# Second mixer of a two-block kernel: one projection chunk moved ahead of the low-rank matmuls, weight splits moved ahead of the token shifts, four small pieces of arithmetic moved between engines

## The reference

```python
h = rms_norm_2(x, mix_norm[l])
p = h @ w_in[l]                                  # 256 x 5296
p_rwkv = token_shift(p[..., :SHIFT_COLS], shift_mu[l])   # u + (prev - u) * mu
# inside rwkv7_mixer, on the shifted columns r, k, v, w_lo, a_lo, g_lo:
w_log = -jax.nn.softplus(-(w0 + jnp.tanh(w_lo) @ w_up)) - 0.5
decay = jnp.exp(-jnp.exp(w_log))
a = jax.nn.sigmoid(a0 + a_lo @ a_up)
g = jax.nn.sigmoid(g_lo) @ g_up
kk = k * k_k
kk = kk / jnp.maximum(jnp.sqrt(jnp.sum(kk * kk, axis=-1, keepdims=True)), 1e-12)
k = k * (1.0 + (a - 1.0) * k_a)
y = rwkv7_recurrence(r, decay, k, v, -kk, kk * a)
```

## Time and profile before

| | |
|---|---|
| median of 3 runs | 1205.22 us (1203.7 to 1205.82) |
| profiled execution, its span | 1203.29 us, 1201.5 us |
| TensorE matmul busy | 1144.5 us, 95% of the span |
| VectorE, ScalarE, GpSimd busy | 771.0, 557.2, 150.0 us |
| mean granted TensorE clock | 0.981 |
| DMA | 188.94 MB, mean 157 GB/s |
| where the mixer's first chunk starts | 699 us of the span, after the last matmuls of the feed-forward |

### The profile page before, as it was taken

How to read it: one execution, slowest core, us unless ns; L and a number is a source line. 1 busy time by engine, 2 the same in 40 slices (tenths; PEclk the granted TensorE clock), 3 DMA queues, 4 the chain that set the end, 5 groups by cost and what they waited for, 6 DMA issues and landing times.

```text
span 1201.5 us, 22075 instructions
## 1 busy us (share of the span) xinstructions
PE 1144.5 (95%) x9584; PEld 1078.9 (90%) x9584; DVE 771.0 (64%) x1042; ACT 557.2 (46%) x660; POOL 150.0 (12%) x112
## 2 busy tenths in 40 slices
PE   7999999989999999899999979999899889999997
PEld 6999999988899999799999968989898778999996
DVE  4888976747686777756455656963257655645554
ACT  6333445473764455654433454422334446434433
POOL 5888760000000000000000000012000000000000
PEclk9999999999999999999999988999999989999999
DMA  8586553344365555555556524323033433565651
GB/s 255 179 290 199 176 175 106 116 161 173 109 208 193 183 201 175 174 175 166 185 176 208 184 97 140 106 75 104 3 106 105 141 106 124 193 213 188 201 163 56
DMA packets 144315, 188.94 MB, mean 157 GB/s; under 512 B 4448, under 2 KB 128921, under 8 KB 144237
## 3 DMA queue, kind: packets, MB, share of 16 engines
q1 hardware_dynamic: 142941, 184.28, 46.3%
q0 software_dynamic: 1104, 3.49, 0.9%
q10 hardware_dynamic: 192, 0.05, 0.0%
HBM read 186.74 MB, written 2.64 MB: 158 GB/s over the span
## 4 chain that ended last, share of the span: by engine, by line
PE 84%; DVE 8%; ACT 5%; issue 2%; ACTq 0%; POOL 0%; DVEq 0%; POOLq 0%
PE bank L1987 19%; PE bank L1988 19%; PE bank L1989 19%; PE bank L2097 5%; PE bank L2098 5%; PE bank L2099 5%; PE bank L551 2%; DVE w_lo L1602 2%; ACT w_hi L1316 2%; PE bank L611 1%; DVE bank L1819 1%; PE bank L2224 1%; ACT sq L1330 1%; DVE x L1676 1%; PE bank L528 1%
## 5 line engine op out<-in xcount | busy, mean ns | idle before, releaser
L1987 PE MATMUL bank<-X_hi,w_hi 128*128 128x256 f32 x1840 | 527.2, 287 | 3.3 <-DVE w_lo L1775 2.9
L1988 PE MATMUL bank<-X_lo,w_hi 128*128 128x256 f32 x1840 | 523.6, 285 | 0.0
L1989 PE MATMUL bank<-X_hi,w_lo 128*128 128x256 f32 x1840 | 523.5, 285 | 0.0
L1316 ACT ACTIVATE w_hi<-w_raw 128x2048 fp32r<-128x2048 f32 x171 | 326.2, 1909 | 176.1 <-PE bank L1989 134.3
L1602 DVE TENSOR_TENSOR w_lo<-w_raw,w_hi 128x2048 fp32r<-128x2048 f32 x146 | 333.7, 2286 | 84.3 <-ACT w_hi L1316 84.0
L1987 PEld LDWEIGHTS bank<-X_hi,w_hi 128*128 128x128 f32 x1840 | 356.1, 194 | 8.6 <-issue 6.8
L1988 PEld LDWEIGHTS bank<-X_lo,w_hi 128*128 128x128 f32 x1840 | 356.2, 194 | 1.2
L1989 PEld LDWEIGHTS bank<-X_hi,w_lo 128*128 128x128 f32 x1840 | 356.0, 193 | 0.0
L1714 DVE TENSOR_TENSOR arena<-bank,rstd 128x512 f32<-128x512 f32 x66 | 45.6, 691 | 185.1 <-PE bank L1989 179.6
L1268 POOL TENSOR_TENSOR w_lo<-w_raw,w_hi 128x2048 fp32r<-128x2048 f32 x24 | 111.3, 4646 | 32.5 <-ACT w_hi L1316 32.4
L2097 PE MATMUL bank<-w_hi,Y_hi 128*128 128x512 f32 x264 | 103.3, 391 | 1.2 <-DVE Y_lo L1742 1.2
(11 more groups left out here) (285 smaller groups left out, 1291.9 us busy)
## 6 DMA issues: line engine op xcount, KB each, us to landing
w_raw<-in_ffn_w_dram SPq DMA_DIRECT2D x66, 1024.0 KB, 5.2
w_raw<-in_w_in_dram SPq DMA_DIRECT2D x53, 1024.0 KB, 5.1
w_raw<-in_w_up_dram SPq DMA_DIRECT2D x22, 1024.0 KB, 5.0
w_raw<-in_w_down_dram SPq DMA_DIRECT2D x11, 1024.0 KB, 4.9
w_raw<-in_w_out_dram SPq DMA_DIRECT2D x8, 1024.0 KB, 4.8
w_raw<-in_conv_pw_w_dram SPq DMA_DIRECT2D x4, 1024.0 KB, 4.9
w_raw<-in_w_attn_out_dram SPq DMA_DIRECT2D x2, 1024.0 KB, 5.1
w_raw<-in_rwkv_proj_dram SPq DMA_DIRECT2D x2, 1024.0 KB, 4.9
```

Of the source, the lines that this page charges most:

```text
L1316: a.activation(w_hi[slot][:, :], raw[slot][:, :], ACT.Copy).then_inc(S["w_hi"], told.one("w_hi"))
L1987: pe.matmul(o, wh, xh, start=start, stop=False, skip_group_check=True)
L1988: pe.matmul(o, wh, xl, start=False, stop=False, skip_group_check=True)
L1989: return pe.matmul(o, wl, xh, start=False, stop=stop, skip_group_check=True)
```

## The change

Only the order and the owner of some work in the mixer's start change; the matmuls and their sizes are the same.

1. TensorE: `columns(B0 + 2)` moves ahead of the low-rank matmuls; decay and rate matmuls alternate; the gate's matmuls come straight after B0+3; head sums move behind B0+4, the turned factors behind B0+5, the forget matmul behind B0+6, the bonus behind B_FOX+1.
2. VectorE and ScalarE: `split` of B0+3 and later stands ahead of other work; a dummy Tanh and a dummy Sqrt load the function tables ahead of need.
3. The factor -exp(-0.5) goes from a VectorE multiply (L911) into the `scale` of the three exponentials.
4. ScalarE squares k with `scale` k_k and does k_a * rate + kept (four Identity each); VectorE's L907 and L954 go; L950 becomes four `scalar_tensor_tensor` reading k and PSUM.
5. GpSimd does the subtraction of L918.

```diff
@@ pe_mixer
             columns(B0, fresh=turn_late_half)
             columns(B0 + 1, midway=spread)
+            columns(B0 + 2)
             pe.wait_ge(S["lora_landed"], 64)
             pe.wait_ge(S["lora_act"], 3)
             for t in range(HT):
-                mm = pe.matmul(bank[6 + t // 2]..., lora_w[0:32, 0, ...], lora_act[0:32, 0, :], ...)
-            mm.then_inc(S["decay_in"], told.one("decay_in"))
-            for t in range(HT):
-                mm = pe.matmul(bank[4 + t // 2]..., lora_w[32:64, 0, ...], lora_act[32:64, 0, :], ...)
-            mm.then_inc(S["rate_in"], told.one("rate_in"))
-            columns(B0 + 2)
+                decay = pe.matmul(bank[6 + t // 2]..., lora_w[0:32, 0, ...], lora_act[0:32, 0, :], ...)
+                rate_mm = pe.matmul(bank[4 + t // 2]..., lora_w[32:64, 0, ...], lora_act[32:64, 0, :], ...)
+            decay.then_inc(S["decay_in"], told.one("decay_in"))
+            rate_mm.then_inc(S["rate_in"], told.one("rate_in"))
             columns(B0 + 3)
-            pe.wait_ge(S["kk_squared"], 1)
-            head_sums(early)
             pe.wait_ge(S["decay_read"], HT)
...
             columns(B0 + 4)
+            pe.wait_ge(S["kk_squared"], HT)
+            pe.wait_ge(S["rstd"], state["rstd"])
+            head_sums(early)
+            columns(B0 + 5)
             pe.wait_ge(S["rate_read"], HT)
             pe.wait_ge(S["factors"], 1)
             turn_factors(early, 4)
-            columns(B0 + 5)
+            columns(B0 + 6)
             pe.wait_ge(S["forget"], 1)
...
-            columns(B0 + 6)
             columns(B_FOX)
+            columns(B_FOX + 1)
             pe.wait_ge(S["g_read"], 2)
             pe.wait_ge(S["rk_ready"], 1)
...
-            columns(B_FOX + 1)
             columns(B_FOX + 2)
@@ act_mixer
+            split(B0 + 3)
+            a.activation(small[:, 62:63], ones[:, 0:1], ACT.Tanh)
             act.wait_ge(S["lora_shifted"], 1)
...
-            split(B0 + 3)
+            split(B0 + 4)
...
-            split(B0 + 4)
-            act.wait_ge(S["kk_raw"], HT)
-            a.activation(flat(early), flat(kk), ACT.Square).then_inc(...)
             split(B0 + 5)
+            act.wait_ge(S["rate_read"], HT)
+            for t in range(HT):
+                a.activation(rate_scaled[:, t, :], rate[:, t, :], ACT.Identity, bias=kept[:, t:t + 1],
+                             scale=col("rwkv_k_a_2", t)).then_inc(S["rate_read"], told.one("rate_read"))
+            act.wait_ge(S["shifted"], HT)
+            for t in range(HT):
+                a.activation(early[:, t, :], k_s[:, t, :], ACT.Square, scale=col("rwkv_k_k_2", t)).then_inc(...)
             split(B0 + 6)
...
+            a.activation(small[:, 62:63], ones[:, 0:1], ACT.Sqrt)
             split(B0 + 7)
+            act.wait_ge(S["head_sums"], 1)
+            a.activation(head_col, bank[3][:, 256:272], ACT.Sqrt, bias=eps[:, 3:4], scale=1.0).then_inc(...)
             act.wait_ge(S["sums"], 1)
-            a.activation(flat(dec_prev), flat(dec_prev), ACT.Exp).then_inc(S["decays"], told.one("decays"))
+            a.activation(flat(dec_prev), flat(dec_prev), ACT.Exp, scale=-EXP_HALF).then_inc(
+                S["decays"], told.one("decays"))
...
@@ gpsimd
+            pool.wait_ge(S["decay_summed"], HT)
+            g.tensor_tensor(flat(dec_prev), flat(dec_inv), flat(dec), ALU.subtract).then_inc(
+                S["sums"], told.one("sums"))
```

More of the change, by code:

```diff
@@ L332, in block_pair @@
         early = region(17414, HT, T)
+        rate_scaled = b_dec
         forget = region(18440, T)
@@ L736, in act_mixer @@
                 S["lora_act"], told.one("lora_act"))
-            split(B0 + 3)
-            for ready, b, dst, gain, name in (("decay_in", 6, dec, "rwkv_w0_2", "decay_read"),
+            split(B0 + 4)
+            for ready, b, dst, gain, done in (("decay_in", 6, dec, "rwkv_w0_2", "decay_read"),
                                               ("rate_in", 4, rate, "rwkv_a0_2", "rate_read")):
@@ L904, in dve_mixer @@
             shifted_columns(B0 + 1)
+            split(B0 + 4)
             shifted_columns(B0 + 2)
-            for t in range(HT):
-                v.tensor_scalar(kk[:, t, :], k_s[:, t, :], col("rwkv_k_k_2", t), None, ALU.mult).then_inc(
-                    S["kk_raw"], told.one("kk_raw"))
+            split(B0 + 5)
+            shifted_columns(B0 + 3)
             dve.wait_ge(S["decay_read"], HT)
-            v.tensor_scalar(flat(dec), flat(dec), -EXP_HALF, None, ALU.mult).then_inc(
-                S["dve_step"], told.one("dve_step"))
-            dve.wait_ge(S["dve_step"], told.value("dve_step"))
             for t in range(HT):
                 v.tensor_tensor_scan(dec_inv[:, t, :], resets[:], dec[:, t, :], 0.0, ALU.mult, ALU.add).then_inc(
[L916 to L920, removed]
+                    S["decay_summed"], told.one("decay_summed"))
             def factors(least, dst, count):
@@ L947, in dve_mixer @@
             dve.wait_ge(S["factors_turned"], 1)
[L948 to L952, removed]
             for t in range(HT):
-                v.tensor_scalar(early[:, t, :], rate[:, t, :], col("rwkv_k_a_2", t), kept[:, t:t + 1], ALU.mult,
-                                ALU.add).then_inc(S["dve_step"], told.one("dve_step"))
-                dve.wait_ge(S["dve_step"], told.value("dve_step"))
-            v.tensor_tensor(flat(k_s), flat(k_s), flat(early), ALU.mult).then_inc(S["dve_step"], told.one("dve_step"))
+                v.scalar_tensor_tensor(out=kk[:, t, :], in0=k_s[:, t, :], scalar=col("rwkv_k_k_2", t),
+                                       in1=bank[4 + t // 2][:, t % 2 * T:t % 2 * T + T], op0=ALU.mult,
+                                       op1=ALU.mult).then_inc(S["dve_step"], told.one("dve_step"))
             dve.wait_ge(S["dve_step"], told.value("dve_step"))
+            dve.wait_ge(S["rate_read"], 2 * HT)
+            v.tensor_tensor(flat(k_s), flat(k_s), flat(rate_scaled), ALU.mult).then_inc(
+                S["dve_step"], told.one("dve_step"))
             v.tensor_tensor(flat(rate), flat(rate), flat(kk), ALU.mult).then_inc(S["dve_step"], told.one("dve_step"))
             dve.wait_ge(S["dve_step"], told.value("dve_step"))
-            shifted_columns(B0 + 5)
+            split(B0 + 8)
+            shifted_columns(B0 + 6)
             for t in range(HT):
```

32 lines of the change are left out of this document (16 added, 16 removed).

## The result

The changed kernel takes 1199.2 us (median of 8 runs, 1193.05 to 1202.83), the kernel before 1207.0 on the same chip (8 runs, 1203.7 to 1212.97). The ratio is 0.9925, with an interval of 0.9905 to 0.9945: 9.1 us faster, 6.6 to 11.5.

The account below looks back on a forecast made before the run. TensorE, on 84% of the span, bounds the kernel, with VectorE nearly as busy in this stretch. `decayed` 12.1 us earlier, less 1.7 for a clock fall, gains 10.4: 1205.2 - 10.4 = 1194.8 us, range 1191.0 to 1199.5.

Parts of the forecast that it names:

- The wait: TensorE ahead of the low-rank matmuls: the wait of 5.73 us goes, with `lora_act` complete 1.5 us before it is wanted.
- The clock after it: TensorE behind that wait: full clock from there on, where chunks B0+2 and B0+3 had lost 2.3 us.
- The low-rank matmuls: Decay and rate matmuls, alternated: 2.5 us instead of 5.55, a saving of 3.05, between 0.5 and 3.75.
- The gate and the second fall: Gate 5.0 us at full clock; one clock fall behind it, 3.4 us long, costing 1.7; the earlier fall cost 3.2.
- the rival to which I gave 0.20: Clock falls as long as before, or twice: 3.2 or 4.7 us lost, gain 8.9 to 7.4, 1196.3 to 1197.8; chance 0.20.
- a sign of error that I had named: The forecast is wrong if the clock is at 0.5 for more than 7 us between 716 and 760.
- VectorE and `decayed`: VectorE waits 2.2 us for the bonus sums; `decayed` comes 7.3 later, at 769.9; TensorE waits 1.6 for it.
- The sum: `decayed` 12.1 us earlier without a clock fall, less 1.7 for one fall: gain 10.4, time 1194.8.
- the 770 to 772 that I had named: Sign in the profile: chunk scores start near 770 to 772, behind a wait of about 1.6 us for VectorE.
- What was costed at nothing: Multiply L911, GpSimd subtraction (2.3 to 2.6 us, cover 4) and ScalarE's Identity and Square steps (cover 8): no cost.
- The chances: Probabilities given: faster by over 0.2% 0.91, within 0.2% 0.05, slower 0.04, beside a chance for each rival.

Follow-up runs that it names:

- e1: The changed kernel with chunk B0+2 put back behind the low-rank matmuls; ratio 0.998 to the kernel before.
- e4: The kernel before with only chunk B0+2 moved ahead of the low-rank matmuls; ratio 0.9982 to the kernel before.
- e6: The changed kernel with the gate's eight matmuls in two pieces of four, the second behind B0+6; ratio 0.9887 to the kernel before.
- e5: The changed kernel with VectorE's bonus product moved behind the two decay products; ratio 0.9896 to the kernel before.
- e2: The changed kernel's order with all arithmetic back on its old engine and in its old form; ratio 0.9935 to the kernel before.
- e3: The kernel before, in its old order, with only the changed arithmetic; ratio 1.0007 to the kernel before.
- e8: The changed kernel with four decay matmuls and then four rate matmuls, not alternated; ratio 0.993 to the kernel before.
- e9: The changed kernel with later bonus product and gate in two pieces (e7), but all arithmetic in its old form; ratio 0.9873 to the kernel before.
- e10: e7 with the bonus product moved once more, to just ahead of the copy of `decayed`'s last factors; ratio 0.9874 to the kernel before.
- e7: The changed kernel with the edits of e5 and e6 together; ratio 0.9863 to the kernel before, median 1189.08 us.

## Why the prediction was right, and where it was not

Forecast 1194.8, a gain of 10.4; measured 9.1, with an interval (6.6 to 11.5) that holds both. The range held the time, but 1199.2 is only 0.3 us inside its end at 1199.5: the forecast counts from 1205.2, the median of three runs, and in eight runs the kernel before took 1207.0. That the absolute time stayed inside is in part luck; the size of the gain is what the prediction got right, and where most of it comes from.

- **The wait.** Right. TensorE goes from B0+2 to the low-rank matmuls without a pause, `lora_act` is complete at 716.05, 1.6 us ahead (forecast 1.5).
- **The clock after it.** Right: no stretch at 1.2 GHz where the first of the earlier trace rows was. In e1 wait and fall came back together, and in e4 the clock was low for 17.1 us from a wait ahead of head sums and gate.
- **The low-rank matmuls.** 1.92 where I took 2.5: the overlap is complete, the end of my bounds at 1.8.
- **The gate and the second fall: the term that was mis-sized.** I gave the fall 3.4 us of length and 1.7 of cost, half of what it was before. It lasted 6.8 as before, began in the gate and not behind it, and cost (731.37 - 725.57) - 5.0 = 0.8 in the gate and (739.53 - 731.37) - 5.75 = 2.4 in B0+4: 3.2. My reason, that head sums no longer stand ahead of the gate, was not enough: the gate alone brings a fall, and e6 takes it away by cutting the gate. The 3.4 that I took does occur, in e5, behind the gate; the other four profiles with the gate in one piece show 6.8, and what decides between them isn't shown. By its own sum the rival to which I gave 0.20 (as long as before, gain 8.9, 1196.3) comes nearer to the measured 8.8 and 9.1 than my 10.4. It was close to a sign of error that I had named: 6.8 us at the low clock between 716 and 760, where more than 7 was to count as wrong.
- **VectorE and `decayed`.** Right in kind: VectorE waited 2.96 for the bonus sums (forecast 2.2, before the fall), TensorE 1.74 for `decayed` (1.6). The 0.54 inside the scores I had not seen. From bonus sums to `decayed` 7.3 us, as forecast.
- **The sum.** Counted from the rstd matmuls, as if before started at 707.64, `decayed` came 1.6 us later than the forecast: 1.5 more for the fall, 0.7 for full chunks, most of which took a little more than 5.75 (741.21 to 747.06 is 5.85), 0.6 less for the low-rank matmuls. So the scores started at 775.13, or 773.3 with the 1.85 us taken off by which the mixer began later, behind the 770 to 772 that I had named. The 8.8 measured in the stretch is the forecast 10.4 less these 1.6, close to the 9.1 of the timed runs.
- **What was costed at nothing** was worth nothing, both ways (e2, e3). The GpSimd subtraction took 4.34 where I said 2.3 to 2.6; the cover hid it: from 731.68 it ended at 736.02, and ScalarE asked for it at 741.7, 5.7 us later (I had 4).
- **The chances.** Those listed add up to 0.90 for faster and 0.06 for within, not to 0.91 and 0.05; nothing hangs on it.

What stays open is how much clock an execution loses behind the stretch. Over the ten traces from before to e8, the time behind `decayed` is 414.0 us plus 0.37 for each us at 1.2 GHz, which correlates at 0.96 (with e9 and e10 413.8, 0.39 and 0.94). That 0.37 is less than the 0.5 I read off one place; that not all of that time is bound by TensorE would explain it, but isn't shown. The changed kernel and e2, which differ in arithmetic alone, both had 31 us of it and e7 17.4; whether the order in the mixer's start has a part in that, I didn't test.

## What to carry to other kernels

A wait of the bounding engine costs more than its length where the clock falls behind it: in e1_third_back 4.2 us of idleness cost 7.5, and one moved call gave them back, but only with the splits ahead brought forward and the next waits cleared (0.75 us alone). Look for falls without idleness too, in or right behind a block of matmuls with few rows, and try to cut the block in two with full ones between (3.5 us here). Relieving an engine that waits anyway gives nothing: look for the engine that the relieved one feeds, and check that it would have waited. And when you sum what an engine can still take, count all its waits in the stretch, and the time that another engine takes from it, not the two largest (e9).

## What the runs showed of the hardware

**GpSimd and VectorE hinder each other, and in every case seen here the one that began second paid.** The GpSimd subtraction and a VectorE split, in the changed kernel and in e3_arith_only (GpSimd's timeline, then for e3 VectorE's):

```profile
731.68 4.34 POOL L1294 TENSOR_TENSOR arena<-arena 128x1024 f32<-128x1024 f32 x1 [494.05 <-DVE arena L921]
```

```profile
734.92 2.37 POOL L1290 TENSOR_TENSOR arena<-arena 128x1024 f32<-128x1024 f32 x1 [497.14 <-DVE arena L919]
```

```profile
735.95 3.49 DVE L1603 TENSOR_TENSOR w_lo<-w_raw,w_hi 128x2048 fp32r<-128x2048 f32 x1 [1.11 <-ACT w_hi L1317]
```

In the changed kernel the split began at 731.52, 0.16 us ahead, and took its usual 2.27; the subtraction took 4.34. In e3 the subtraction began 1.03 ahead and took 2.37; the split took 3.49 instead of 2.29. The Trainium skill, GPSIMD Engine Reference, 1. Specifications, says that GpSimd shares its interfaces to SBUF with VectorE and contends with VectorE instructions that read two SBUF inputs, as this split does. The two rows agree; that the first one keeps the way is what they show: the split first in seven traces (4.32 to 4.35 for the subtraction in changed, e1, e5, e6, e7, e8, e10), the subtraction first in e3. In both orders the second took about as much longer as the two overlapped: 2.0 of 2.1 us, 1.2 of 1.3. In e6, e7 and e10 VectorE's next product of two SBUF inputs (L885) began 3.1 us behind the subtraction and took 1.79 instead of 0.69, while the read-out ahead of it (L1649), which takes one input from PSUM, took its usual 0.69 beside it.

**Matmuls of 32 rows overlap, and not only with their neighbour.** In e8 the rate matmuls, four decay matmuls behind, have records that lie beside those of the decay matmuls: L486's first at 716.86, L483's last at 717.50; in e4 718.91 and 719.56. Still e8's form cost 1.0 us more than the alternated one, where the pairs started 0.01 us apart.

**The clock falls without idleness.** At 729.5, after 11.9 us in which TensorE was busy throughout (the row of 717.60 above), it fell inside the gate; in e6 the same eight matmuls in two halves let it stand.
